# Differential attention: when ScalarE runs the exponentials of a pair's second unit, and when VectorE makes the low parts of later queries

## The reference, cut to what matters

```python
def diff_mixer(q, k, v, lam_p, sub_g, lam_init, bias_tab, pos, idx, valid):
    lam = jnp.exp(jnp.sum(lp[0] * lp[1])) - jnp.exp(jnp.sum(lp[2] * lp[3])) + lam_init
    def one_block(i):                      # 128 queries
        logits = jnp.einsum('bqhcd,bkhcd->bchqk', qb, k) * scale + bias[None, None]   # c: two components
        p = masked_softmax(logits, mask)
        attn = p[:, 0] - lam * p[:, 1]
        return jnp.einsum('bhqk,bkhd->bqhd', attn, v)
    out = rms_norm_2(out, sub_g) * (1.0 - lam_init)
```

## Time and profile before

| | us |
|---|---|
| median of three runs | 1901.83 |
| the three runs | 1897.15, 1903.69, 1901.83 |
| the profiled execution | 1900.31 |
| span of its trace | 1898.5 |
| TensorE, VectorE, ScalarE, GpSimd busy | 1815.4, 1018.2, 732.4, 295.0 |

### The profile page before, as it was taken

The page is one execution under the profiler, slowest core; times in us unless marked ns, Lnnn a source line. Parts: engine busy times, 40 slices in busy tenths (PEclk is TensorE's granted clock), DMA queues, the critical chain, the costliest instruction groups (busy, mean ns, idle before and its releaser), DMA issues.

```text
span 1898.5 us, 22254 instructions
## 1 busy us (share of the span) xinstructions
PE 1815.4 (96%) x8983; PEld 1456.3 (77%) x8983; DVE 1018.2 (54%) x1518; ACT 732.4 (39%) x1220; POOL 295.0 (16%) x235
## 2 busy tenths in 40 slices
PE   8999999999999998989999999899878999999998
PEld 5778876788888876778888888787656788888887
DVE  6777845444454366357777722574365534444322
ACT  4433343332334444344444422445356533222221
POOL 2013501011212040141111100500100101111100
PEclk9999999999999999999999999999978899999999
DMA  5222322232224421122222222231300122222221
GB/s 190 89 78 89 101 89 78 78 112 98 91 93 153 143 94 40 67 78 88 90 90 100 83 106 100 91 110 69 106 12 32 56 91 98 89 100 89 100 89 56
DMA packets 49829, 171.13 MB, mean 90 GB/s; under 512 B 5882, under 2 KB 8570, under 8 KB 49600
## 3 DMA queue, kind: packets, MB, share of 16 engines
q1 hardware_dynamic: 45216, 155.69, 23.8%
q0 software_dynamic: 3936, 13.51, 2.1%
q10 hardware_dynamic: 576, 0.52, 0.1%
HBM read 165.51 MB, written 4.19 MB: 89 GB/s over the span
## 4 chain that ended last, share of the span: by engine, by line
PE 82%; DVE 6%; ACT 5%; issue 4%; POOL 2%; DMA 0%; SPq 0%; DVEq 0%; POOLq 0%; ACTq 0%
PE ps L377 26%; PE ps L379 25%; PE ps L378 25%; PE ps L382 3%; PE ps L2600 2%; ACT ws_h L305 1%; POOL sums L424 1%; DVE ws_l L313 1%; PE ps L2617 1%; ACT P L2724 1%; POOL x L1441 1%; DMA x<-in_x 0%; PE ps L2612 0%; DVE tmp L815 0%; ACT x L1144 0%
## 5 line engine op out<-in xcount | busy, mean ns | idle before, releaser
L313 DVE TENSOR_TENSOR ws_l<-raw,ws_h 128x1024 fp32r<-128x1024 f32 x289 | 394.4, 1369 | 522.4 <-ACT ws_h L305 521.9
L377 PE MATMUL ps<-h_h,ws_h 128*128 128x512 f32 (+1 forms) x1448 | 582.3, 402 | 19.4 <-DVE h_l L548 10.3
L379 PE MATMUL ps<-h_h,ws_l 128*128 128x512 f32 (+1 forms) x1448 | 571.2, 394 | 0.0
L378 PE MATMUL ps<-h_l,ws_h 128*128 128x512 f32 (+1 forms) x1448 | 570.9, 394 | 0.0
L305 ACT ACTIVATE ws_h<-raw 128x1024 fp32r<-128x1024 f32 x289 | 303.4, 1054 | 448.9 <-PE ps L379 446.0
L377 PEld LDWEIGHTS ps<-h_h,ws_h 128*128 128x128 f32 x1448 | 276.4, 191 | 93.4 <-issue 16.1
L379 PEld LDWEIGHTS ps<-h_h,ws_l 128*128 128x128 f32 x1448 | 276.6, 191 | 61.6
L378 PEld LDWEIGHTS ps<-h_l,ws_h 128*128 128x128 f32 x1448 | 278.4, 192 | 58.5
L377 PE MATMUL ps<-G_h,ws_h 128*128 128x512 f32 (+1 forms) x374 | 142.9, 382 | 1.1 <-DVE ws_l L313 1.1
L379 PE MATMUL ps<-G_h,ws_l 128*128 128x512 f32 (+1 forms) x374 | 142.6, 381 | 0.0
L378 PE MATMUL ps<-G_l,ws_h 128*128 128x512 f32 (+1 forms) x374 | 142.6, 381 | 0.0
(11 more groups left out here) (437 smaller groups left out, 2418.9 us busy)
## 6 DMA issues: line engine op xcount, KB each, us to landing
raw<-in_ffn_up SPq DMA_DIRECT2D x88, 512.0 KB, 3.2
raw<-in_w_merge SPq DMA_DIRECT2D x36, 512.0 KB, 3.2
raw<-in_ffn_down SPq DMA_DIRECT2D x22, 512.0 KB, 3.2
raw<-in_w_down SPq DMA_DIRECT2D x22, 512.0 KB, 3.2
raw<-in_w_hy SPq DMA_DIRECT2D x12, 512.0 KB, 4.0
raw<-in_w_sc SPq DMA_DIRECT2D x12, 512.0 KB, 3.3
raw<-in_fwd SPq DMA_DIRECT2D x8, 512.0 KB, 3.3
raw<-in_w_naqk SPq DMA_DIRECT2D x8, 512.0 KB, 3.2
```

What stands on the lines that cost most here:

```text
L313: dve.e.tensor_tensor(w.lo, raw[n % NRAW][:], w.hi, ALU.subtract).then_inc(*lo_made.says(("lo", n)))
L377: pe.e.matmul(o, a.hi, b.hi, start=start, stop=False, skip_group_check=True)
L378: pe.e.matmul(o, a.hi, b.lo, start=False, stop=False, skip_group_check=True)
L379: return pe.e.matmul(o, a.lo, b.hi, start=False, stop=stop, skip_group_check=True)
```

## The change

It has two parts, and both only move steps within one engine's order.

In `copies_first`, at the turn of a D pair's first unit, ScalarE now also lets go the held scores of the unit behind it. So the four exponentials of D0.1 are issued in front of the copies of D0.0's transposes instead of behind them, and those of D1.1 in front of the copies of D1.0.

VectorE goes through a list of its own, `queries_behind`: the steps queries 2, 3 and 4 (the low parts of the queries of W0, W1 and W2) are held until the next scores step has been issued. Queries 0 and 1 stay. TensorE and GpSimd, and ScalarE's high parts of the queries, keep their places.

```diff
@@ def copies_first():
             if step[0] in ("turn", "turned"):
-                n = at_unit[step[1]] + (step[0] == "turned") * len(LINE)
+                ahead = step[1][0] == "D" and step[1][2] == 0
+                n = at_unit[step[1]] + (len(LINE) if step[0] == "turned" else ahead)
                 yield from (s for s in held if at_unit[s[1]] <= n)
                 held = [s for s in held if at_unit[s[1]] > n]
             yield step
@@
+    def queries_behind():
+
+        held = None
+        for step in ORDER:
+            if step[0] == "queries" and step[1] > 1:
+                held = step
+                continue
+            yield step
+            if held and step[0] == "scores":
+                yield held
+                held = None
+
     def attention_dve():
@@
-        for what, u, c in ORDER:
+        for what, u, c in queries_behind():
             if what == "scores":
                 scores(u, c)
```

## The result

The changed kernel takes 1891.93 us in the median of five runs (1890.76 to 1895.03), the kernel before 1903.69 in the median of the five beside it (1897.15 to 1909.36). The ratio is 0.9955, with a 95% interval from 0.9937 to 0.9973: faster by 8.6 us, between 5.1 and 12. The two medians themselves lie 11.8 us apart, near the upper end of this interval. In a second comparison, of ten runs beside 23, the ratio is 0.9970 (0.9955 to 0.9984), 5.7 us, between 3.0 and 8.6. So the change makes the kernel faster. The first interval lies above the 4.5 us that were forecast, the second has them in it. The median lies in the range, 5.4 us under the forecast of 1897.3.

The account below looks back on a forecast made before the run. The prediction took TensorE, busy 96% of the span, as the bound, with engines waiting in a ring in the D pairs. Waits of 2.0 + 2.5 = 4.5 us, clock 0, took 1901.83 to 1897.3 us; range 1891 to 1902.5.

Parts of the forecast that it names:

- Part 1 in pair 0: D0: unit 1's exponentials ahead of unit 0's copies on ScalarE bring the product for M2 and later steps 2.0 us sooner.
- the walk: Following the D pairs' waits instruction by instruction on each engine's timeline, with before's durations; it gave 4.5 us.
- Queries 2 and 3: Pair 0 and the start of D1: moving these low parts behind the next scores on VectorE gains 0.
- Queries 4 and pair 1: D1: scores of unit 1 start 1.37 us sooner without queries 4 ahead; with part 1, pair 1 gives 2.5 us.
- The sum of the waits: Both D pairs: 2.0 us in pair 0 and 2.5 in pair 1 make 4.5 us at before's clock.
- The clock, 0: TensorE's granted clock, the open term: 0 taken as likeliest, the middle of gains and losses, with both ends kept.
- the three low stretches named: Clock at 0.50 at 1386 to 1393, 1407 to 1410 and 1417 to 1423 us, costing 2.2, 1.5 and 3.0 us.
- the clock stays up: Rival, chance 0.37: shrunken gaps in the D pairs keep low stretches away; 1895.8 down to 1890.6, around 1893.
- the last condition of the prediction: Sign of error: low stretches from 1386 on at other places and lengths, the shift changing at them, not at waits.
- Given back: Rival, chance 0.12: ScalarE's copies or VectorE's sum in pair 1 take over; 1899.8 with only pair 0's gain, 1901.8 with none.
- copies late: Rival: unit 0's copies wait up to 2.02 us behind unit 1's exponentials in each pair; counted under the given-back chance.
- slower: Rival, chance 0.09: the W stage's 1434 to 1461 us falls to low clock; 7.5 us more, 1909.3.

Follow-up runs that it names:

- part 2 alone: Changed kernel with ScalarE's order put back as it was, VectorE's low parts of queries 2 to 4 still held: ratio 0.9982 (0.9967 to 0.9998).
- queries4_only: Changed kernel with only queries 4 held behind the scores on VectorE, queries 2 and 3 back where they were: ratio 0.9960 (0.9945 to 0.9976).
- each part alone: Changed kernel with only ScalarE's exponentials moved, ratio 0.9988, or with only VectorE's queries moved, ratio 0.9982.
- the fillers: Extra matmuls whose result nobody reads, put in TensorE's gaps: 104 gave 0.9988 on the kernel before, 0.9941 on the changed; 62 gave 0.9966 and 0.9916.
- after_fit: Changed kernel with 62 extra matmuls that nobody reads, sized to its TensorE gaps: 1885.97 us, ratio 0.9916 (0.9902 to 0.9930).
- the fillers in front: after_fit with 26 more extra matmuls, before D0's first scores and the first projection step behind them: ratio 0.9919 (0.9902 to 0.9936).
- before_filled: Kernel before with 104 extra matmuls that nobody reads, in front of six steps where TensorE stands idle: ratio 0.9988 (0.9977 to 0.9999).

## Why the prediction was right, and where its size was off

- *Part 1 in pair 0, 2.0 us.* Right: 2.02 at each of the three places named, the product for M2, the scores of unit 3, and TensorE's second half of them (19.97 us behind the first score before, 17.95 changed). The cover was 2.48 us against the 2.4 of the walk. But that the rest of the pair hangs on it did not hold in this trace: the scores of D1.1 start 33.47 us behind the first score, 33.32 before. In between TensorE waits once more, before the transposes of D0.3, for VectorE's difference of unit 3; the walk did not have this wait. The rows, before and changed:

```profile
1398.18 0.63 PE L2617 MATMUL ps<-ident,P 128*128 128x128 f32 x4 [2.71 <-DVE P L2859]
```

```profile
1396.33 0.88 PE L2617 MATMUL ps<-ident,P 128*128 128x128 f32 x4 [2.14 <-DVE P L2873]
```

  These transposes come 29.55 us behind the first score before, 28.10 changed: 1.45 us are left there. The two rows below, of before and changed, run from the second half of the scores to the scores of D1.1. The work is the same and the idle time falls from 2.7 to 2.1, but the clock is 0.67 instead of 0.84, and 2.7 us of busy time came in, 1.6 of them in a low stretch at 1396 to 1400. That is a matter of the execution: in the second traces the scores of D1.1 stand 36.29 us behind the first score before and 33.58 changed, and with part 2 alone 36.12.

```profile
1388.60:1401.95 13.35, 10.64 (x82) 8.12 (x82) 8.72 (x28) 6.77 (x19) 0.00 (x0) 0.84 0.00 0
```

```profile
1386.18:1401.70 15.52, 13.38 (x82) 9.99 (x82) 8.72 (x28) 6.83 (x19) 0.00 (x0) 0.67 0.00 0
```

- *Queries 2 and 3, nothing.* Right, by queries4_only.
- *Queries 4 and pair 1, 2.5 us.* Right: 2.6 at the full clock; 1.25 for each part alone, with a short low stretch. The scores of D1.1 start 1.22 us after VectorE's step before them, without queries 4 between, and TensorE's wait is 1.74; 1.7 was forecast.
- *The sum of the waits, 4.5.* Right: 4.7 us of idle time in the mean of the traces. Part 1 gives 2.9 of it by its trace and part 2 0.8; that this is 1 us short of the sum is within the spread of the idle times of one kernel (15.6 to 16.7).
- *The clock, 0.* This is the term that was mis-sized. I took it as the middle of gains and losses; it was 4.1 us in the mean of the traces, never under 2.4 for any pair of them (100.1 less 97.6). By time it is less certain: beyond the waits' 4.5, the first comparison leaves 4.1 and the second 1.2. Of the three low stretches named, the first stayed, and the two of pair 1 are gone: from the scores of D1.1 to the first score of W0 nothing is low in any of the three traces of the changed kernel, nor in that of queries4_only, while both traces of the kernel before and those of each part alone have low stretches there. From the mean of D0 to the first score of W0 alone, the kernel before and then the changed one:

```profile
1416.44:1427.57 11.13, 10.75 (x62) 7.74 (x62) 3.92 (x12) 6.48 (x14) 0.00 (x0) 0.69 0.01 2
```

```profile
1412.11:1420.35 8.24, 7.76 (x62) 5.53 (x62) 4.63 (x15) 6.57 (x14) 0.00 (x0) 1.00 0.01 3
```

  The same 62 instructions take 7.76 us instead of 10.75, 3.0 us; for 1417 to 1423 the prediction had 3.0. So the prices were right, and the weighing was not: the gains stood behind named gaps that shrink, the losses behind nothing in particular. The rival "the clock stays up", with 0.37 and a time from 1890.6 to 1895.8, is what came, and not the forecast as summed, with 0.42; the median is in the range because the range kept this rival. Low stretches also came at other places, as the one at 1396, so the last condition of the prediction was met too: the shift grew at them and not only at the waits. Why shorter gaps leave fewer low stretches is argued from this and from the fillers; how the clock is decided is not shown.
- *What a low stretch costs.* I held that it costs less than half its length where TensorE also waits. The same interval of the kernel before, with fillers, took 14.41 us at 0.88 and 13.00 at 1.00. At 0.88, 24% of 14.41 us, 3.5 us, is low, and it cost 1.41, which is 0.41 of its length. The rule of the Trainium skill (TensorE: Matmul & The Clock Gate, section Terms) has one half, an estimate of 1.7. Where TensorE is busy nearly all the time, as from 1416.44 to 1427.57 (0.69, so 6.9 us low for 3.0 of busy time), it is 0.43, so one half is an upper end in both.
- *Given back, copies late, slower.* None came. But the cover in pair 1 was thin: ScalarE ended unit 1's exponentials and then waited 0.64 us for the transposes, where the walk had 2: the transposes came sooner than in the walk, with no low stretch in front of them. A loss of the kind named for the clock did come, at 1396.

The Trainium skill (TensorE: Matmul & The Clock Gate, section What's actually happening) says that activity releases the throttle. That agrees with after_fit, whose clock in the stretch is 0.94 against 0.84, and not with the fillers in front, which changed nothing; no run here shows why.

## What to carry to other kernels

Where engines wait for each other in a ring, put an engine's ready work ahead of its next wait, and follow the gain step by step to what is late next: the walk had 4.5 us of waits, and the traces have 4.7 in the mean. A gap that closes on TensorE can be worth more than its length, since the work behind it may run at the full clock (here 5.7 and 8.6 us by time for 4.5 of waits); weigh that as a gain on its own, and read it by splitting one stretch of equal work into idle and busy time. Where a gap can't be closed, matmuls that nobody reads, sized to fit it, brought another 0.4 to 0.5% here (0.9916 against 0.9955 and 0.9970).

## What the runs showed of the hardware

The two traces of the same kernel meet their low stretches at different steps: pair 1's scores-to-mean interval takes 14.49 us in one and 14.87 in the other, in which more of it is low. One trace can't tell what the clock costs: in three of the changed kernel the same work, from the first score of D0 to the last values of W2, takes 95.3 to 97.6 us of busy time. And the clock can be at 0.50 for 13 us while TensorE is busy all the time. That stretch is gone in after_fit, where 10 fillers stand in the gap in front of it; but in before_filled one as long stands at an earlier place, and it begins where 8 fillers run:

```profile
1463.21:1476.83 13.62, 13.62 (x66) 9.73 (x64) 4.17 (x18) 5.33 (x21) 0.00 (x0) 0.50 0.00 1
```

So a filled gap made low stretches rarer here and ruled none out.
